# Streaming only the 64 query columns a level uses in the tree products of a gated linear recurrence

## The chip, the cores and the metric

The kernel runs on one core of one Trainium2 chip. The metric is the device time of one execution in microseconds (us); for a kernel it is the median of its runs.

## The reference, cut to what matters

One transformer block on a sequence of 1024 tokens of width 1024, all in float32: an RMS norm, one input projection, a sparse attention mixer (8 heads of 64), a gated linear recurrence (4 heads, keys and values of 128, chunks of 64 tokens in the reference), an output projection, and an MLP of width 4096. The change lies in the recurrence:

```python
def step(state, xs):                      # one chunk of C tokens, per head
    qc, kc, vc, lc = xs                   # lc = log of the forget gate f, kc = 1 - f
    bc = jnp.cumsum(lc, axis=2)
    diff = jnp.where(causal[:, :, None], bc[:, :, :, None, :] - bc[:, :, None, :, :], -jnp.inf)
    a = jnp.einsum('bhtd,bhsd,bhtsd->bhts', qc, kc, jnp.exp(diff))
    o = jnp.einsum('bhtd,bhdv->bhtv', qc * jnp.exp(bc), state) + jnp.einsum('bhts,bhsv->bhtv', a, vc)
    b_last = bc[:, :, -1:, :]
    state = jnp.exp(b_last[:, :, 0, :])[..., None] * state + jnp.einsum('bhsd,bhsv->bhdv', kc * jnp.exp(b_last - bc), vc)
    return state, o
```

The matrix `a` says how strongly query t of a chunk sees key s, with the product of all gates between s and t in it, separately for each of the 128 features.

## The kernel before, in words

The stages follow each other: input projection (to about 332 us of the profiled execution), attention (to about 648 us), the recurrence (to about 746 us), then output projection and MLP. Each engine (TensorE, called PE in the profile, with its weight loads PEld; VectorE, DVE; ScalarE, ACT; GpSimd, POOL; SyncE, SP) has its own instruction stream in program order, and they meet at semaphores.

The recurrence takes chunks of 128 tokens (8 chunks, `NT`), 4 heads (`HH`). It never forms the 128x128x128 decay. It builds `a` as a binary tree of seven levels. At level l the tokens are cut into blocks of b = 2^l; two neighbouring blocks form a pair, and the level fills in those entries of `a` whose key lies in the first block of a pair and whose query lies in the second. For that, `hgrn_q` (`hq`) and `hgrn_k` (`hk`) hold queries and keys that already have the gates up to the pair's border multiplied in. Features stand on the partitions and tokens on the free axis, so one product of a chunk and head is one TensorE matmul: stationary operand `hk[:, c, head]` (128 features x 128 keys), moving operand `hq[:, c, head]` (128 features x 128 queries), result 128 keys x 128 queries in PSUM. The operands are float32, and each such matmul stands in the trace as two weight loads and two matmuls, so 16 records are one pair of chunks (2 chunks x 4 heads x 2), which fills two PSUM banks.

- Units. A unit `u` is one pair of chunks `cp` at one level, or on the diagonal: `level_unit(l, cp)` = 4 + 4 l + cp; units 0 to 3 are the diagonal. `pair_banks(u)` gives unit u two of the eight banks, in a ring of 4 units (`A_RING`). The diagonal products (moving operand `fm`, called `hgrn_qf`) come first, 64 records, then 7 levels x 4 units x 16 = 448 records (L2122, called at L2146).
- Waits of PE ahead of a unit of level l: the bank pair must have been merged (`A_dve` or `A_act`, unit u - 4), and for every second unit `q_up` and `k_up`, which say that VectorE has multiplied the gates of level l - 1 into `hq` and `hk` of half the chunks (`grp`). The two units of one half are called a group below: 32 records.
- VectorE, for each level and half: wait for the two units of the level (`A_full`), then multiply the gates into the second blocks of `hq` (L1589) and the first blocks of `hk` (L1590), combine the gates (L1591), and for levels 0 to 3 merge the two units into `hgrn_A` with a predicated copy (L1599). That copy reads only the columns of second blocks, `[:, :, :, b:2 * b]`.
- ScalarE merges levels 4 to 6 with plain copies (L1164), again only from second blocks' columns.
- After level 6, PE transposes `hk` (L2157) and runs the chunks one after the other: state products (L2190) and outputs (L2167, L2168).

The helper that the change uses existed before and VectorE used it at L1586 and L1587:

```python
def blocks_of(ap, b):
    v = ap.rearrange("p (n c) -> p n c", c=2 * b)
    return v[:, :, 0:b], v[:, :, b:2 * b]
```

Of the kernel before, what the change touches and what calls it, by code (L numbers as in the profile page):

```python
# [31 lines left out]
P = 128  # L32
# [11 lines left out]
HH = 4  # L44
# [210 lines left out]
def program(nc, x, attn_norm, w_in, q_norm, k_norm, cmp_pe_k, cmp_w1_k, cmp_w2_k, cmp_pe_v, cmp_w1_v,  # L255
# [5 lines left out]
    def sb(name, shape, dt, offset=None):  # L261
        if offset is None:
            n = 2 if dt == BF16 else 4
            for k in shape[1:]:
                n *= k
            n = (n + 31) // 32 * 32
            offset = at["small"]
            at["small"] += n
        return nc.alloc_sbuf_tensor_at(name, list(shape), dt, offset=base + offset)
# [37 lines left out]
    hk = sb("hgrn_k", [P, NT, BW], F32, 0)  # L307
    hq = sb("hgrn_q", [P, NT, BW], F32, 16384)
# [263 lines left out]
    def root_act(act, bufs, width):  # L572

        sums, _, log, root = bufs
        n = roots["act"] = roots["act"] + 1
        act.activation(log, sums, ACT.Ln, bias=eps[:, 0:1], scale=1.0 / width).then_inc(logs_ready, 1)
        act.wait_ge(logs_ready, n)
        act.activation(root, log, ACT.Exp, scale=-0.5).then_inc(root_ready, 1)
# [67 lines left out]
# [4 lines that stand above are left out]
# [13 lines left out]
    def level_unit(l, cp):  # L663

        return 4 + 4 * l + cp

    def pair_banks(u):

        return ps[:, 2 * (u % A_RING):2 * (u % A_RING) + 2, :].rearrange("p a x -> p (a x)")
# [122 lines left out]
    with nc.Block() as block:  # L792
# [565 lines left out]
        def _(dve):  # L1358
# [216 lines left out]
            for l in range(len(LEVELS)):  # L1575
                b = 1 << l
                for grp in range(2):
# [5 lines left out]
                    else:  # L1583
                        dve.wait_ge(q1_done, 4)
                        dve.wait_ge(k_done, 4)
                    _, q2 = blocks_of(flat(hq[:, 4 * grp:4 * grp + 4, :]), b)  # L1586
                    k1, _ = blocks_of(flat(hk[:, 4 * grp:4 * grp + 4, :]), b)  # L1587
                    f_ = products(l, grp).rearrange("p (n c) -> p n c", c=2)
# [303 lines left out]
        def _(pe):  # L1892
            pe.wait_ge(e_loaded, 80)
            nc.tensor.transpose(ps[:, 7, 0:GAIN_ROWS], gain_rows[:], eye[0:GAIN_ROWS, 0:GAIN_ROWS]).then_inc(gainsT, 1)
            for t in range(NT // 2):
                pe.wait_ge(x_loaded[t], 16)
                for k in range(KC):
                    if t == 0 and k == 7:
                        pe.wait_ge(gains_out, 1)
                    ins = nc.tensor.transpose(ps[:, k, t * P:(t + 1) * P], x_in[:, t, k * P:(k + 1) * P], eye[:])  # L1900
                    if t == 3:
                        ins.then_inc(rowsT_done, 1)
            for k in range(KC):
                pe.wait_ge(rows_low, k + 1)
                for t in range(NT // 2, NT):
                    if k == 0:
                        pe.wait_ge(x_loaded[t], 16)
                    ins = nc.tensor.transpose(ps[:, k, (t % 4) * P:(t % 4 + 1) * P], x_in[:, t, k * P:(k + 1) * P], eye[:])
# [208 lines left out]

            def product(u, c, rhs):  # L2120
                for h in range(HH):
                    ins = nc.tensor.matmul(pair_banks(u)[:, (HH * (c % 2) + h) * P:(HH * (c % 2) + h + 1) * P],  # L2122
                                           hk[:, c, h * P:(h + 1) * P], rhs(h), start=True, stop=True)
                return ins

            for cp in range(4):
                pe.wait_ge(k_done, cp + 1)
                for c in range(2 * cp, 2 * cp + 2):
                    ins = product(cp, c, lambda h: fm[:, 0, c, h, :])
                ins.then_inc(A_full, 1)  # L2130
            for l in range(len(LEVELS)):
                b = 1 << l
                for cp in range(4):
                    u = level_unit(l, cp)
                    if l == 0:
                        pe.wait_ge(q1_done, cp + 1)
                    elif cp % 2 == 0:
                        pe.wait_ge(q_up, 2 * (l - 1) + cp // 2 + 1)
                        pe.wait_ge(k_up, 2 * (l - 1) + cp // 2 + 1)
                    old = u - A_RING + 1  # L2140
                    if old > MERGED_BY_DVE:
                        pe.wait_ge(A_act, old - MERGED_BY_DVE)
                    else:
                        pe.wait_ge(A_dve, old)
                    for c in range(2 * cp, 2 * cp + 2):
                        ins = product(u, c, lambda h: hq[:, c, h * P:(h + 1) * P])  # L2146
                    ins.then_inc(A_full, 1)

            def kT(c):
# [31 lines left out]
            for c in range(NT):  # L2181
                if c < 3:
                    kT(c + 4)
                if c < NT - 1:
# [3 lines left out]
                    for h in range(HH):  # L2188
                        cols = slice(h * P, (h + 1) * P)
                        ins = nc.tensor.matmul(ps[:, c % 2, cols], hKT[:, c, cols], hv[:, 0, c, cols], start=True, stop=True)  # L2190
# [109 lines left out]
            for k in range(last):  # L2300
                g, c = divmod(k, NCPS)
# [36 lines left out]
```

## Time and profile before

| What | Value |
|---|---|
| median of 3 runs | 1470.96 us (1465.0 to 1474.64) |
| the profiled execution's own time | 1472.83 us |
| its span in the trace | 1471.0 us |
| PE busy, PEld busy | 1428.5 us (97%), 1222.5 us (83%) |
| DVE busy, ACT busy | 870.2 us (59%), 623.0 us (42%) |
| mean granted TensorE clock | 0.992 of full |

The span is the time from the first to the last instruction of the profiled execution, and 1.8 us lie around it. Times of rows count from the span's start. PE's busy time includes pipelined matmuls whose modelled ends overlap the next one's start; how fast PE gets on is read from the distance between starts. PEclk is the granted clock: 1.00 is 2.4 GHz and 0.50 is 1.2 GHz.

### The profile page before, as it was taken

The numbers are of one execution on the slowest core, as the hardware profiler recorded it, in microseconds if no ns is written. First come the engines' busy times: TensorE is split into PE (matmuls) and PEld (weight loads), VectorE is DVE, ScalarE is ACT, GpSimd is POOL, SyncE is SP. The second block draws the span as 40 slices with busy tenths as digits, with TensorE's granted clock in tenths as the row PEclk, the third lists the DMA queues.
The fourth block names the chain that finished last, engine by engine and source line by source line (L and its number), as shares of the span: only waits on it lengthen the run. The fifth ranks groups of instructions, "written<-read, shape, count | busy, mean of one in ns | idle before, by whom it ended". The sixth has DMA issues, their size and how long they took to land.

```text
span 1471.0 us, 21626 instructions
## 1 busy us (share of the span) xinstructions
PE 1428.5 (97%) x7950; PEld 1222.5 (83%) x7950; DVE 870.2 (59%) x1630; ACT 623.0 (42%) x1235; POOL 161.5 (11%) x178
## 2 busy tenths in 40 slices
PE   7999999999999999998999989999999999999999
PEld 6888888878888888898987868888888788888887
DVE  3002681106666776669784586666666598569764
ACT  5014302215554545460440467755555554444441
POOL 2433343521000000000242000000000000000000
PEclk9999999998999999999999999999999999999999
DMA  5211114200000000012011014444444966643332
GB/s 176 61 47 51 51 36 122 72 7 1 1 2 1 1 2 1 1 44 115 30 51 36 30 36 165 158 152 157 157 158 139 327 206 191 213 127 100 93 115 86
DMA packets 78254, 129.42 MB, mean 88 GB/s; under 512 B 8973, under 2 KB 26826, under 8 KB 78154
## 3 DMA queue, kind: packets, MB, share of 16 engines
q1 hardware_dynamic: 77968, 128.01, 27.3%
q8 instruction: 63, 1.03, 0.3%
q14 instruction: 37, 0.30, 0.1%
q10 hardware_dynamic: 186, 0.08, 0.0%
HBM read 94.51 MB, written 33.55 MB: 87 GB/s over the span
## 4 chain that ended last, share of the span: by engine, by line
PE 87%; DVE 8%; ACT 2%; issue 2%; DMA 1%; SPq 0%; DVEq 0%; ACTq 0%
PE ps L518 64%; PE ps L2102 6%; PE ps L2062 4%; PE ps L2077 4%; PE ps L2122 3%; PE ps L2096 1%; PE ps L2046 1%; PE ps L1935 1%; DVE negmax L1492 1%; PE ps L2067 1%; DMA x_in<-in_x_dram 1%; PE ps L757 1%; DVE q_stack L1485 1%; PE ps L624 0%; DVE hgrn_A L1599 0%
## 5 line engine op out<-in xcount | busy, mean ns | idle before, releaser
L518 PE MATMUL ps<-mlp_w_high,hidden_high 128*128 128x512 f32 x448 | 174.3, 389 | 0.0
L518 PE MATMUL ps<-mlp_w_low,hidden_high 128*128 128x512 f32 x448 | 174.3, 389 | 0.0
L518 PE MATMUL ps<-mlp_w_high,hidden_low 128*128 128x512 f32 x448 | 174.3, 389 | 0.0
L518 PE MATMUL ps<-w_high,hT_high 128*128 128x512 f32 (+1 forms) x448 | 170.5, 380 | 0.8 <-ACT cmp_v L1072 0.7
L518 PE MATMUL ps<-w_low,hT_high 128*128 128x512 f32 (+1 forms) x448 | 168.1, 375 | 0.0
L518 PE MATMUL ps<-w_high,hT_low 128*128 128x512 f32 (+1 forms) x448 | 168.0, 375 | 0.0
L2102 PE MATMUL ps<-nsa,probs_T 128*128 128x64 f32 x1056 | 138.2, 275 | 0.0
L1664 DVE TENSOR_TENSOR mlp_w_low<-mlp_w_raw,mlp_w_high 128x512 fp32r<-128x512 f32 x112 | 77.1, 690 | 98.3 <-ACT mlp_w_high L1200 98.3
L1299 ACT ACTIVATE mlp_w_high<-mlp_w_raw 128x512 fp32r<-128x512 f32 x112 | 70.6, 630 | 148.2 <-PE ps L518 148.2
L2102 PEld LDWEIGHTS ps<-nsa,probs_T 128*128 128x128 f32 x1056 | 129.5, 193 | 0.0
L1744 DVE TENSOR_TENSOR mlp_w_low<-mlp_w_raw,mlp_w_high 128x512 fp32r<-128x512 f32 x112 | 77.0, 688 | 65.8 <-ACT mlp_w_high L1299 65.8
L518 PE MATMUL ps<-x1T_t_high,mlp_w_high 128*128 128x512 f32 x256 | 100.8, 394 | 6.2 <-issue 5.4
L1122 ACT ACTIVATE probs<-ps,negmax 128x640 f32<-128x640 f32 (+7 forms) x128 | 89.4, 699 | 29.5 <-DVE negmax L1492 29.5
L518 PE MATMUL ps<-x1T_t_high,mlp_w_low 128*128 128x512 f32 x256 | 100.6, 393 | 0.0
L518 PE MATMUL ps<-x1T_t_low,mlp_w_high 128*128 128x512 f32 x256 | 100.6, 393 | 0.0
L1492 DVE TENSOR_REDUCE negmax<-ps 128x1 f32<-128x640 f32 (+7 forms) x128 | 89.3, 701 | 18.5 <-PE ps L2067 17.9
L518 PEld LDWEIGHTS ps<-mlp_w_high,hidden_low 128*128 128x128 f32 x448 | 84.1, 188 | 17.6
L518 PEld LDWEIGHTS ps<-mlp_w_high,hidden_high 128*128 128x128 f32 x448 | 84.1, 188 | 17.5
L518 PEld LDWEIGHTS ps<-mlp_w_low,hidden_high 128*128 128x128 f32 x448 | 84.1, 188 | 17.3
L518 PEld LDWEIGHTS ps<-w_high,hT_high 128*128 128x128 f32 x448 | 84.1, 188 | 17.1 <-DVE hT_low L1364 1.6
L1134 ACT ACTIVATE probs_T<-ps 128x128 f32<-128x128 f32 (+3 forms) x129 | 53.2, 430 | 102.9 <-PE ps L2077 101.7
L518 PEld LDWEIGHTS ps<-w_high,hT_low 128*128 128x128 f32 x448 | 84.1, 188 | 15.2
(234 smaller groups left out, 2893.1 us busy)
## 6 DMA issues: line engine op xcount, KB each, us to landing
hidden_raw<-hidden_pieces SPq DMA_DIRECT2D x112, 256.0 KB, 2.7
mlp_w_raw<-in_w_mlp_in_dram SPq DMA_DIRECT2D x32, 512.0 KB, 4.2
hidden_pieces<-hidden SPq DMA_DIRECT2D x64, 256.0 KB, 2.8
mlp_w_raw<-in_w_mlp_out_dram SPq DMA_DIRECT2D x64, 256.0 KB, 4.3
w_raw<-in_w_in_dram SPq DMA_DIRECT2D x56, 256.0 KB, 2.7
hidden_pieces<-hidden_s SPq DMA_DIRECT2D x48, 256.0 KB, 2.2
x_in<-in_x_dram SPq DMA_DIRECT2D x8, 512.0 KB, 7.3
w_raw<-in_w_out_dram SPq DMA_DIRECT2D x16, 256.0 KB, 2.8
```

Source lines behind the costliest of these rows:

```text
L518: ins = nc.tensor.matmul(out_ap, a_hl[i], b_hl[j], start=first and n == 0, stop=last and n == 2, skip_group_check=onto_a_sum_already_read)
L757: ins = nc.tensor.transpose(ps[:, bank0 + f, q * P:(q + 1) * P], source(f, q), eye[:])
L1122: act.activation(o, sv, ACT.Exp, bias=negmax[:, j % NEGMAX:j % NEGMAX + 1], accum_out=rsums[:, hh % 2, t, int(kind == "win"):int(kind == " ...
L1134: act.activation(pT[:, it.groups[m]["pt"], 0:n], ps[:, T_BANK + m % 2, 0:n], ACT.Copy).then_inc(t_act, 1)
L1299: act.activation(ring_slot(W2R, k)[0], w2_source(k), ACT.Copy).then_inc(w2_highs, 1)
L1492: dve.tensor_reduce(negmax[:, j % NEGMAX:j % NEGMAX + 1], sv, AX if len(sv.shape) == 2 else mybir.AxisListType.XY, ALU.max, negate=True).t ...
L1664: dve.tensor_tensor(W1_L[:, s, :, :], w1_source(*IN_ORDER[k]), W1_H[:, s, :, :].bitcast(F32), ALU.subtract)\
L1744: dve.tensor_tensor(wl, w2_source(k), wh.bitcast(F32), ALU.subtract).then_inc(w2_lows, 1)
L2062: ins = nc.tensor.matmul(o, QT[:, hh % 2, t * P:(t + 1) * P], k_[:, br, hh // HPG:hh // HPG + 1, tiles[0] * P + b * (w // nb):tiles[0] * P ...
L2077: ins = nc.tensor.transpose(ps[:, T_BANK + m % 2, q * P:(q + 1) * P], probs[:, j % P_SLOTS, (u["first"] + q) * P:(u["first"] + q + 1) * P] ...
L2102: ins = nc.tensor.matmul(ps[:, O_BANK + it.pair(j) % 2, c:c + DK], lhs, nsa[:, tiles[n], v0 + hh // HPG * DK:v0 + (hh // HPG + 1) * DK], s ...
L2122: ins = nc.tensor.matmul(pair_banks(u)[:, (HH * (c % 2) + h) * P:(HH * (c % 2) + h + 1) * P], hk[:, c, h * P:(h + 1) * P], rhs(h), start=T ...
```

## The change

The products of the levels get a function that narrows both the moving operand and the place in the bank: `blocks_of(ap, b)[1]`, the second block of each pair. A level then streams 64 of the 128 query columns: every second column at level 0, runs of 2, 4, 8, 16, 32 at levels 1 to 5, and the last 64 in one run at level 6. The stationary operand stays 128 x 128. The columns in between are no longer written; VectorE and ScalarE did not read them at these levels. The diagonal products still stream all 128. The number of instructions, their order and all waits are unchanged.

```diff
-            def product(u, c, rhs):
+            def product(u, c, rhs, part=lambda ap: ap):
                 for h in range(HH):
-                    ins = nc.tensor.matmul(pair_banks(u)[:, (HH * (c % 2) + h) * P:(HH * (c % 2) + h + 1) * P],
-                                           hk[:, c, h * P:(h + 1) * P], rhs(h), start=True, stop=True)
+                    ins = nc.tensor.matmul(part(pair_banks(u)[:, (HH * (c % 2) + h) * P:(HH * (c % 2) + h + 1) * P]),
+                                           hk[:, c, h * P:(h + 1) * P], part(rhs(h)), start=True, stop=True)
                 return ins
...
-                        ins = product(u, c, lambda h: hq[:, c, h * P:(h + 1) * P])
+                        ins = product(u, c, lambda h: hq[:, c, h * P:(h + 1) * P], lambda ap: blocks_of(ap, b)[1])
```

## Rows read from the trace of the kernel before

**Rows 1.** The page: busy time by engine, and the granted clock in 40 slices

```profile
PE 1428.5 (97%) x7950; PEld 1222.5 (83%) x7950; DVE 870.2 (59%) x1630; ACT 623.0 (42%) x1235; POOL 161.5 (11%) x178
...
PEclk9999999998999999999999999999999999999999
```

**Rows 2.** The chain that ended last, 600 to 800 us: start, us, what

```profile
649.62 12.63 PE ps L2122 x96
...
687.33 3.81 PE ps L2122 x32
691.14 25.45 PE ps L2122 x224
716.62 1.22 DVE hgrn_q L1589
```

**Rows 3.** Timeline of 644 to 735 us: PE's records of the recurrence

```profile
658.49 7.31 PE L2122 MATMUL ps<-hgrn_q,hgrn_k 128*128 128x128 f32 x64
...
667.16 3.81 PE L2122 MATMUL ps<-hgrn_q,hgrn_k 128*128 128x128 f32 x32 [1.36 <-DVE hgrn_A L1599]
...
672.83 3.81 PE L2122 MATMUL ps<-hgrn_q,hgrn_k 128*128 128x128 f32 x32 [1.85 <-DVE hgrn_A L1599]
...
677.95 3.81 PE L2122 MATMUL ps<-hgrn_q,hgrn_k 128*128 128x128 f32 x32 [1.31 <-DVE hgrn_A L1599]
...
687.33 29.25 PE L2122 MATMUL ps<-hgrn_q,hgrn_k 128*128 128x128 f32 x256 [0.45 <-DVE hgrn_A L1599]
...
717.35 1.94 PE L2157 MATMUL ps<-eye,hgrn_k 128*128 128x128 f32 x16 [0.77 <-ACT hgrn_A L1164]
```

**Rows 4.** Groups of 658 to 720 us, shapes apart: busy us, mean ns, idle before

```profile
L1599 DVE COPY_PREDICATED hgrn_A<-tree_masks,ps 128x512 f32<-128x512 int32 x16 | 14.8, 997 | 0.0
L1589 DVE TENSOR_TENSOR hgrn_q<-hgrn_q,hgrn_f 128x1024 f32<-128x1024 f32 x12 | 14.7, 1226 | 4.7 <-PE ps L2122 4.7
L1590 DVE TENSOR_TENSOR hgrn_k<-hgrn_k,hgrn_f 128x1024 f32<-128x1024 f32 x12 | 14.5, 1211 | 0.0
L1164 ACT ACTIVATE hgrn_A<-ps 16x128 f32<-16x128 f32 x16 | 4.3, 269 | 38.5 <-DVE hgrn_A L1599 38.3
```

**Rows 5.** The chain of 640 to 650 us: attention's last matmuls of 64 columns

```profile
644.93 2.87 PE ps L2102 x26
```

**Rows 6.** The compression's matmuls, moving operand read with a step of 8 elements

```profile
237.63 7.71 PE L1935 MATMUL ps<-cmp_tokens,cmp_w 128*128 128x130 f32 x32
```

**Rows 7.** Busy time of each stretch, granted clock (PEclk), DMA share, GB/s

```profile
336.50:340.00 3.50, 3.50 (x19) 3.47 (x18) 0.10 (x1) 0.12 (x1) 0.16 (x1) 0.56 0.00 0
340.00:344.20 4.20, 3.36 (x17) 2.80 (x17) 2.79 (x6) 1.99 (x7) 0.00 (x0) 0.50 0.01 4
344.20:347.70 3.50, 3.50 (x19) 3.50 (x19) 0.71 (x3) 0.58 (x3) 0.00 (x0) 0.50 0.00 0
347.70:350.60 2.90, 2.90 (x14) 2.28 (x15) 1.72 (x4) 1.41 (x5) 0.00 (x0) 0.50 0.01 3
350.60:354.00 3.40, 3.40 (x27) 2.84 (x27) 3.22 (x11) 1.98 (x6) 0.00 (x0) 1.00 0.00 0
644.70:647.80 3.10, 3.08 (x29) 2.94 (x26) 0.57 (x4) 0.77 (x2) 0.00 (x0) 1.00 0.00 0
647.80:650.90 3.10, 1.28 (x11) 1.28 (x12) 2.96 (x5) 2.39 (x3) 0.00 (x0) 1.00 0.43 128
650.90:654.30 3.40, 3.40 (x18) 3.40 (x18) 3.34 (x4) 3.37 (x5) 0.00 (x0) 0.51 0.93 308
654.30:658.40 4.10, 4.10 (x39) 4.10 (x38) 2.91 (x3) 4.10 (x15) 0.00 (x0) 0.99 0.10 35
...
672.80:677.90 5.10, 3.81 (x32) 3.65 (x32) 5.10 (x6) 0.00 (x0) 0.00 (x0) 1.00 0.96 374
```

**Rows 8.** Timeline of 341 to 351 us: attention's compressed outputs, 64 columns

```profile
344.28 3.62 PE L2096 MATMUL ps<-cmp_v,probs_T 128*128 128x64 f32 x16
...
347.69 0.42 PE L2077 MATMUL ps<-eye,probs 128*128 128x128 f32 x1
```

## The prediction

> **What bounds the kernel now.** I read four views in this order. The page first: PE is busy for 97% of the span, weight loads for 83%, VectorE for 59%, and the granted clock is full nearly everywhere [rows 1]. That says only that PE's pace matters somewhere. The chain that ended last says where: around the recurrence's products it runs over PE from 649.62 for 96 records (64 of the diagonal, 32 of level 0), then over VectorE, and from 687.33 over PE alone for 32 + 224 records, up to VectorE's gate products at 716.62 [rows 2]. The timeline shows why. From 667 to 687 us each group of 32 PE records takes 3.8 us and then PE idles 1.3 to 1.9 us until a merge of VectorE's frees banks [rows 3]; VectorE has no idle time before its merges, and 4.7 us in all before its gate products [rows 4]. So levels 0 to 2 are VectorE's, though PE's groups take nearly as long, and levels 3 to 6 are PE's: 256 records in 29.25 us. There are 448 such records, 51 us of PE's time, in one stage of 1471 us; the change touches nothing else.
>
> **The pace of these records.** 224 records took 25.45 us [rows 2], 114 ns each, with 128 columns streamed. What does one of 64 columns take? Attention has it, with the same kinds of operands (float32, stationary 128x128): 26 records in 2.87 us, 110 ns [rows 5]. The few ns between them are the waits between units. Half the columns buy nothing, so what limits the pace is not the stream but the load of the stationary operand, which the change leaves alone. The Trainium skill, page "TensorE: Matmul & The Clock Gate", section "LDWEIGHTS (loading the stationary operand)", gives 128 / 1.2 = 107 ns for such a load whatever the moving operand; an estimate by it says the same as the row of 64 columns.
>
> **Term 1: the stream of the 448 records at full clock.** Removed: 64 columns each. Gain 0 by rows 5, as the weight load covers it. If that cover were gone, the most to gain is the idle time that VectorE has before its gate products, 4.7 us [rows 4], since VectorE is then what is late next. At the ends of groups the last result may land some tens of ns sooner; only two such ends lie on the chain where PE hands over for good (662 and 717 us), so I count 0.1 us, which is nothing.
>
> **Term 2: the strided reads and writes.** The nearest row for reading is the compression's matmul: its moving operand has a step of 8 elements, and 32 records of 130 columns take 7.71 us [rows 6]. Taking off the last one's tail of about 0.4 us, 31 steps take 7.3 us, 235 ns each or 1.81 ns per column. 64 such columns would take 116 ns, 4 ns over the 112 of the load. That row has a wider step than any level here (2 elements at level 0, runs from level 1 on), so it is the upper end for reading: 448 x 4 ns = 1.8 us. The lower end is 0: at level 0 the 64 columns touch the same stretch of memory as 128 contiguous ones, and those keep pace with the load. I take 0, because levels 2 to 6 have runs of four columns or more. No row shows a strided write into PSUM. Bound it below by 0 (no reason lets it speed anything up), above by a doubling to about 224 ns at level 0 alone, where single columns are written: 32 records lie on the chain ahead of 662 us, and the other 32 delay level 1; together 64 x 0.11 = 7 us at most, of which the 1.36 us of idle time after it [rows 3] hides some, so about 5.5. I take 0 here too.
>
> **Term 3: the clock.** This is the part where I expect the time to move. The granted clock has two levels in this trace, and it is worth asking what PE had done before each move.
> - It fell from 1.00 to 0.50 near 337 us and near 651 us [rows 7]. Ahead of the second lie 26 records of 64 columns (full clock, though thinly streamed) and then 1.85 us without work between the stages; it fell 3.2 us after the idle time began, with PE busy again with 128-column records.
> - At 0.50, 3.5 us of PE 100% busy did not bring it back: in 344.2 to 347.7 PE and its loads were busy all the time, with 16 records of 64 columns, and the clock stayed at 0.50, through the next stretch too; it was back at 1.00 after matmuls of 384 columns [rows 7, 8].
> - In 650.9 to 654.3 PE was just as busy, at half clock, with 128-column records, and the clock came back at once [rows 7].
> So a PE that is busy with loads is not enough; it is the streamed columns that tell these stretches apart. In the levels, idle gaps of 1.3 to 1.9 us today lie between groups of 128 columns, and the clock holds (672.8 to 677.9 is 1.00 with 3.81 of 5.1 us busy) [rows 7]. After the change the same gaps lie between groups of 64 columns, which is what PE did ahead of the fall at 651. I expect the clock to fall after the gap that ends level 0 (it starts near 665.8): by the 3.2 us seen above, near 669. Then every group is 64-column work at half clock, the very pattern of 344.2 to 347.7 that did not bring the clock back. It should stay at 0.50 until the products end.
>
> What that costs. At half clock the 64-column records stand 3.41 us / 16 = 213 ns apart (344.28 to 347.69) [rows 8]; with the 2 ns for waits between units (114 against 112) 215. Group 1 of level 1 starts at 667.16 at full clock and falls on the way: about 16 records at 112 and 16 at 213 take 5.2 us, so it ends by 672.4, ahead of 672.83, when the banks of the next group come free [rows 3]: nothing lost yet. From there 11 groups are left, 352 records x 0.215 = 75.7 us. VectorE needs per group 2.4 us for the two gate products (1.2 each) and up to 2.4 for two merges or none [rows 4], less than the 6.9 that PE takes, and each group of PE needs only gate products that can run during the other half's group. So no wait is left in it, and PE ends at 672.83 + 75.7 = 748.5 in place of 716.6: +31.9 us. Everything behind waits for it: VectorE's last gate products, the transposes, the chunks. The loads of the output projection's weights are not late today and have only more time.
>
> After the products come transposes and state products of 128 columns, which brought the clock back in 3.4 us at 651. I give it 5 us here, as PE has two short waits at the start [rows 3]; at half pace that loses 2.5 us.
>
> **The sum.** 0 + 0 + 31.9 + 2.5 = +34.4 us. The profiled execution took 1472.83 us (span 1471.0), so it would be 1507.2, span 1505.4. The median of the runs, 1470.96, is 1.9 us lower; on it the forecast is 1505.4 us.
>
> **Rival A: the clock holds.** Then only terms 1 and 2 are left, and the weight load hides both: 1471 us. For it: the gaps keep their length, PE's busy share stays, and the clock held through long runs of 64-column records in attention [rows 5, 7]. Against it: those runs had no idle time, and where one came (647.8) the clock fell. The Trainium skill (same page, "Why this matters for your kernels") names only idle gaps between bursts as what costs the clock, longer ones than any here; by that rule the change would give 1471. The trace disagrees at 651, where a gap of 1.85 us was enough. Chance 0.10.
>
> **Rival B: strided access is dear and the clock is not the matter.** If level 0 alone doubles, +5.5 us, 1476. If all levels but the last, which is one run, went to twice the time, 11 groups less level 6's two would run at about 224: 9 x 32 x 0.11 = +32, near 1503, at full clock. It decides from the point where a record passes the 112 ns of the load; reading by rows 6 gives 116. The Trainium skill has a rule that speaks for it: "SBUF — State Buffer" on cachelines says that any non-contiguous PSUM access slows matmuls significantly. No row here shows it for writes. Chance 0.06, half of it near 1476.
>
> **Rival C: faster, because the stream matters after all.** Then PE finishes the groups of levels 3 to 6 early and VectorE binds: at most its 4.7 us of idle time [rows 4], 1466. Against it rows 5. Chance 0.02.
>
> **How the numbers follow.** The forecast, clock lost until the products end, has 0.82. Its own range: below, if the clock comes back for part of the way (half of the levels spared, 1488); above, level 0 doubled (+5.5), the clock already lost ahead of level 0's first group (32 records x 0.10 = 3.3), a slower return behind (+3), reading at its upper end at levels 0 and 1 (+1): 1518. I take 1488 to 1518; it holds 0.78 of the 0.82, and with the dear half of rival B 0.81 in all. By over 1%, 14.7 us (about what a measurement of this kernel can tell from no change), it is slower in the forecast's case and in the dear half of B, less a little for a clock that comes back soon: 0.83. Within 1%: A, cheap B, C and that little: 0.16. Faster by over 1%: 0.01, since nothing seen could give 15 us.
>
> **What the changed profile would show.** The granted clock at 0.50 from near 669 to near 753 and nowhere else anew; PE's product records 213 ns apart there and 112 in level 0; the idle times of PE before groups gone from level 2 on, and those of VectorE before its gate products grown to 3 us and more each; the stage's end some 32 us later and the stages behind it unchanged in length. Term 1 is right if level 0's 64 records still take about 7.3 us. If that group takes 14 us at clock 1.00, B was right. If the clock stays at 1.00 with the gaps in place, A was, and my reading of the two falls was wrong: something else than columns tells those stretches apart.

## The result

The changed kernel takes 1507.45 us (median, 1502.68 to 1509.85) against 1472.34 us of the kernel before (1465.0 to 1474.97). The ratio is 1.0245, with a 95% interval of 1.0222 to 1.0269: 2.5% slower. The forecast was 1505.4 us, range 1488 to 1518. The profiled execution took 1504.32 us with a span of 1502.4 us, 31.4 more than before.

The page has the same 21626 instructions. PE's busy time rose from 1428.5 to 1466.6 us although it streams fewer columns, VectorE's stayed (871.3 against 870.2), and two slices of the span have about half the clock where [rows 1] had full:

```profile
PE 1466.6 (98%) x7950; PEld 1261.3 (84%) x7950; DVE 871.3 (58%) x1630; ACT 622.9 (41%) x1235; POOL 161.4 (11%) x178
...
PEclk9999999999999999985599999999999999999999
```

PE's timeline of 653 to 751 us in the changed kernel shows the recurrence's products:

```profile
653.81 7.26 PE L2122 MATMUL ps<-hgrn_q,hgrn_k 128*128 128x64 f32 x64
662.43 82.16 PE L2122 MATMUL ps<-hgrn_q,hgrn_k 128*128 128x64 f32 x384 [1.36 <-DVE hgrn_A L1599]
745.36 4.50 PE L2157 MATMUL ps<-eye,hgrn_k 128*128 128x128 f32 x20 [0.77 <-ACT hgrn_A L1164]
```

Level 0's 64 records take 7.26 us where they took 7.31 [rows 3]: at full clock half the columns buy nothing. Then the four groups with idle time ahead and the run of 256 of [rows 3] have become one run of 384 records in 82.16 us, 214 ns each, without an idle moment. The chain of this stretch follows PE all the way where it followed VectorE for 25 us before [rows 2]:

```profile
662.43 82.17 PE ps L2122 x384
744.62 0.60 ACT hgrn_A L1164
```

The windows of the changed kernel (start and end, length, PE busy, PEld busy, DVE, ACT, POOL, granted clock, DMA share, GB/s) show the clock and what PE did around its moves:

```profile
644.80:648.00 3.20, 1.44 (x12) 1.44 (x13) 3.12 (x5) 2.55 (x3) 0.00 (x0) 1.00 0.43 150
653.80:661.00 7.20, 7.20 (x66) 7.13 (x64) 4.79 (x6) 3.76 (x11) 0.00 (x0) 1.00 0.00 1
661.00:661.80 0.80, 0.07 (x1) 0.00 (x0) 0.80 (x2) 0.00 (x0) 0.00 (x0) 1.00 0.00 0
661.80:668.70 6.90, 6.27 (x30) 6.30 (x30) 6.90 (x7) 0.00 (x0) 0.00 (x0) 0.50 0.13 45
668.70:744.60 75.90, 75.88 (x356) 75.69 (x355) 39.34 (x51) 9.05 (x27) 0.00 (x0) 0.50 0.13 52
744.60:750.60 6.00, 5.25 (x25) 5.28 (x26) 5.59 (x8) 0.59 (x1) 3.17 (x4) 0.50 0.04 9
750.60:765.00 14.40, 14.40 (x131) 14.40 (x131) 9.44 (x27) 4.76 (x9) 4.18 (x5) 1.00 0.21 71
```

Level 0 runs at full clock. In the 1.36 us of idle time behind it the clock falls to 0.50 (1.2 GHz) and stays there for 89 us, with PE busy nearly all the time (its only idle moment of note is the 0.77 us ahead of the transposes). It comes back 6 us after the last product, once 128-column transposes and state products run. VectorE, which had 4.7 us of idle time before its gate products [rows 4], now waits 36.5 us (groups of 658 to 750 us):

```profile
L1589 DVE TENSOR_TENSOR hgrn_q<-hgrn_q,hgrn_f 128x1024 f32<-128x1024 f32 x12 | 14.7, 1225 | 36.5 <-PE ps L2122 36.5
```

**The 31.4 us, stage by stage,** from the starts of PE's records in the two profiled executions:

| Stretch | before | changed | difference |
|---|---|---|---|
| start to level 0's first record | 658.49 | 653.81 | -4.68 |
| level 0 to the first transpose (L2157) | 58.86 | 91.55 | +32.69 |
| to the output projection's first matmul (L518) | 29.14 | 30.97 | +1.83 |
| to the MLP's first matmul | 98.27 | 99.88 | +1.61 |
| to the end | 626.2 | 626.2 | 0 |

The first row is not the change's: attention ended 3.1 us earlier in that execution, where the clock's fall at 337 us lasted 6.8 us in place of 13.7; and the fall at 651 us [rows 7] did not happen (1.00 from 644.8 to 661 above), though PE did the same work. The fourth is a short fall of the clock behind idle time in the output projection. The work and the idle time are the same in both kernels, but in one of the two profiles the clock fell:

```profile
770.00:778.00 8.00, 5.95 (x28) 4.66 (x27) 7.66 (x18) 0.00 (x0) 1.96 (x2) 1.00 0.21 66
778.00:790.00 12.00, 12.00 (x62) 10.21 (x61) 5.52 (x8) 2.42 (x4) 1.82 (x2) 1.00 0.01 1
```

These are windows of the kernel before; the same stretch of the changed kernel:

```profile
800.00:808.00 8.00, 5.95 (x29) 4.70 (x28) 7.48 (x17) 0.00 (x0) 1.96 (x2) 1.00 0.20 66
808.00:820.00 12.00, 12.00 (x55) 10.23 (x54) 5.61 (x8) 2.59 (x4) 0.46 (x1) 0.86 0.01 1
```

Such a fall is worth 1.6 us. Whether it belongs to the change is open: of the thirteen profiles of this document seven have it (this one, contig64, narrow012, wide3, square6, tiles056 and tilesall), and none of the five whose levels take the 58.8 to 58.9 us of the kernel before. The stage itself is the measure below: "levels" is the time from level 0's first record to the first transpose, 58.86 us before and 91.55 after.

### The profile page after: what moved, and what is told of

It is laid out like the page before. It is cut to its first block, busy times and chain, and to the rows that moved or that the text cites. A ratio compares the mean times of both kernels' runs of the same rounds, so it can differ in the third digit from the quotient of the medians.

```text
span 1502.4 us, 21626 instructions
## 1 busy us (share of the span) xinstructions
PE 1466.6 (98%) x7950; PEld 1261.3 (84%) x7950; DVE 871.3 (58%) x1630; ACT 622.9 (41%) x1235; POOL 161.4 (11%) x178
## 4 chain that ended last, share of the span: by engine, by line
PE 89%; DVE 6%; ACT 2%; issue 2%; DMA 1%; SPq 0%; ACTq 0%; DVEq 0%
PE ps L518 63%; PE ps L2122 6%; PE ps L2102 6%; PE ps L2062 4%; PE ps L2077 3%; PE ps L1935 1%; PE ps L2096 1%; PE ps L2046 1%; DVE negmax L1492 1%; PE ps L2067 1%; DMA x_in<-in_x_dram 1%; PE ps L757 1%; DVE q_stack L1485 1%; PE ps L624 0%; DVE hgrn_vg L1633 0%
## 5 line engine op out<-in xcount | busy, mean ns | idle before, releaser
L518 PE MATMUL ps<-mlp_w_high,hidden_high 128*128 128x512 f32 x448 | 174.4, 389 | 0.0
L518 PE MATMUL ps<-mlp_w_high,hidden_low 128*128 128x512 f32 x448 | 174.4, 389 | 0.0
L518 PE MATMUL ps<-mlp_w_low,hidden_high 128*128 128x512 f32 x448 | 174.4, 389 | 0.0
L518 PE MATMUL ps<-w_high,hT_high 128*128 128x512 f32 (+1 forms) x448 | 171.1, 382 | 0.8 <-ACT cmp_v L1072 0.7
L518 PE MATMUL ps<-w_low,hT_high 128*128 128x512 f32 (+1 forms) x448 | 168.6, 376 | 0.0
L518 PE MATMUL ps<-w_high,hT_low 128*128 128x512 f32 (+1 forms) x448 | 168.3, 376 | 0.0
L518 PE MATMUL ps<-x1T_t_high,mlp_w_high 128*128 128x512 f32 x256 | 100.8, 394 | 6.3 <-issue 5.4
L518 PE MATMUL ps<-x1T_t_high,mlp_w_low 128*128 128x512 f32 x256 | 100.6, 393 | 0.0
L518 PE MATMUL ps<-x1T_t_low,mlp_w_high 128*128 128x512 f32 x256 | 100.6, 393 | 0.0
L518 PEld LDWEIGHTS ps<-w_high,hT_high 128*128 128x128 f32 x448 | 84.5, 189 | 17.1 <-DVE hT_low L1364 1.6
L518 PEld LDWEIGHTS ps<-mlp_w_high,hidden_high 128*128 128x128 f32 x448 | 84.1, 188 | 17.6
L518 PEld LDWEIGHTS ps<-mlp_w_high,hidden_low 128*128 128x128 f32 x448 | 84.1, 188 | 17.5
L518 PEld LDWEIGHTS ps<-mlp_w_low,hidden_high 128*128 128x128 f32 x448 | 84.1, 188 | 17.3
L518 PEld LDWEIGHTS ps<-w_high,hT_low 128*128 128x128 f32 x448 | 84.4, 188 | 15.2
L518 PEld LDWEIGHTS ps<-w_low,hT_high 128*128 128x128 f32 x448 | 84.5, 189 | 14.6
```

What stands on the lines that cost most here:

```text
L518: ins = nc.tensor.matmul(out_ap, a_hl[i], b_hl[j], start=first and n == 0, stop=last and n == 2, skip_group_check=onto_a_sum_already_read)
```

## The experiments

All runs were compared with the kernel before on the same chip; the kernel before took 1468.65, 1472.64, 1474.53 and 1472.69 us in the four sets.

**Is it the stride or the number of columns?** Two kernels split the change in two. The first keeps 64 columns and takes the stride away; it leaves out most entries of levels 0 to 5:

```diff
-ins = product(u, c, lambda h: hq[:, c, h * P:(h + 1) * P], lambda ap: blocks_of(ap, b)[1])
+ins = product(u, c, lambda h: hq[:, c, h * P:(h + 1) * P], lambda ap: ap[:, P // 2:P])
```

> At every level the products stream the last 64 of the 128 query columns in one contiguous run, into the last 64 columns of the bank, so most entries of the matrix are wrong at levels 0 to 5; instructions and waits are those of the changed kernel. Theory of columns (the clock falls because few columns are streamed around the idle time after level 0, and stays down): as slow as the changed kernel, +35 us on the kernel before, about 1507, with 213 ns between records from level 1 on at clock 0.50. Theory of strides (the strided view is what slows the records): no stride is left, so the time is that of the kernel before, 1472, at clock 1.00.

Measured: 1507.34 us, ratio 1.0259 (1.0221 to 1.0296). Levels 91.55 us, to the hundredth those of the changed kernel:

```profile
651.32 7.26 PE L2122 MATMUL ps<-hgrn_q,hgrn_k 128*128 128x64 f32 x64
659.94 82.15 PE L2122 MATMUL ps<-hgrn_q,hgrn_k 128*128 128x64 f32 x384 [1.36 <-DVE hgrn_A L1599]
```

The second keeps the strides and streams all 128 columns:

```diff
+ins = product(u, c, lambda h: hq[:, c, h * P:(h + 1) * P], lambda ap: ap.rearrange("p (n a c) -> p a n c", a=2, c=b))
```

> At every level all 128 columns are streamed, first blocks of all pairs first and then second blocks, each with the stride of the level, and written to the same places, so the result is the same. Theory of columns: the time of the kernel before, 1472 (within 3 us), clock 1.00, 112 ns between records, at level 0 too. Theory of strides: slower by at least as much as the changed kernel, 1507 or more, with long records at clock 1.00.

Measured: 1469.76 us, ratio 1.0001 (0.9978 to 1.0024), levels 58.93 us. PE's timeline of this kernel, level 0, then the groups of levels 1 and 2:

```profile
662.27 7.42 PE L2122 MATMUL ps<-hgrn_q,hgrn_k 128*128 128x128 f32 x64
671.00 3.87 PE L2122 MATMUL ps<-hgrn_q,hgrn_k 128*128 128x128 f32 x32 [1.31 <-DVE hgrn_A L1599]
676.66 3.86 PE L2122 MATMUL ps<-hgrn_q,hgrn_k 128*128 128x128 f32 x32 [1.80 <-DVE hgrn_A L1599]
681.78 3.81 PE L2122 MATMUL ps<-hgrn_q,hgrn_k 128*128 128x128 f32 x32 [1.26 <-DVE hgrn_A L1599]
```

Against 7.31, 3.81 and 3.81 us [rows 3] the stride costs 0.11 us on 64 records at level 0, 0.05 to 0.06 on 32 at level 1, and nothing from level 2 on; the idle time behind takes it up. That holds for reading and writing together. With 64 columns it costs nothing at all: level 0 takes 7.26 us in the changed kernel and in contig64. The strides are cleared as a cause; the number of columns is it. (They are not shown to be free. The output projection's records of 512 columns, of the form fp32r, start 0.227 us apart at full clock; at that pace 128 columns take 57 ns, and twice that, 113 ns, would barely show beside the 112 ns of the load. These are estimates, and level 0 here runs at 113.5 ns against 111.7 before, so a stride that doubles the stream is not excluded.)

**Does it take idle time as well as few columns?** 64 columns at levels 4 to 6 only, where PE has no idle time:

```diff
+... lambda ap: blocks_of(ap, b)[1] if l >= 4 else ap)
```

> 64 columns only at levels 4 to 6, where PE has no idle time; 128 at levels 0 to 3. Theory that narrow streams cost the clock only together with idle time: clock stays 1.00, time of the kernel before, 1472 (within 2 us), since the weight load hides the stream. Rival, that narrow streams alone cost the clock: 192 records x 0.102 us = +20 and some 2 us for the return, 1494.

Measured: 1472.29 us, ratio 1.0014 (0.9988 to 1.004), levels 58.79 us; the clock held (windows of this kernel):

```profile
681.60:710.80 29.20, 29.16 (x256) 28.89 (x256) 24.54 (x36) 9.04 (x27) 0.00 (x0) 1.00 0.00 1
```

From level 3 on (`l >= 3`), with 0.45 us of idle time ahead of the first narrow group:

> The changed kernel with 128 columns at levels 0 to 2: 64 columns from level 3 on. Ahead of level 3 PE idles 0.45 us, ahead of its second group 0.2 us, later never. Theory (it takes narrow records and more than a short idle time together): clock stays 1.00, 1472. Rival (0.45 us of idle time among narrow records is enough): it falls near 690 us and stays down to the end of the levels, some 230 records x 0.102 = +23 and 2 for the return, 1497.

Measured: 1472.67 us, ratio 0.9995 (0.997 to 1.002), levels 58.81 us at clock 1.00. Narrow records by themselves neither cost the clock nor gain a thing. The other way round, 64 columns at levels 0 to 2 only:

```diff
+... lambda ap: blocks_of(ap, b)[1] if l < 3 else ap)
```

> 64 columns only at levels 0 to 2, where PE idles between groups; 128 at levels 3 to 6. Theory of columns: the clock falls after level 0, groups of levels 1 and 2 take 128 x 0.213 = 27.3 us from 667.2 on, 7.1 us longer than to 687.3, then 128-column records at half clock bring it back in 3 to 7 us, which costs 2.5 us: +9.6, 1482 (1478 to 1485). Rival, that a clock once lost stays lost as long as this stage lasts whatever is streamed: +34, 1506.

Measured: 1482.32 us, ratio 1.0068 (1.0041 to 1.0096), which is +10.0 us; levels 66.31 us, +7.45, and the profile has the 1.6 us in the output projection too. Windows:

```profile
658.90:666.20 7.30, 7.30 (x67) 7.20 (x65) 4.66 (x5) 2.48 (x6) 0.00 (x0) 1.00 0.00 1
666.20:670.30 4.10, 2.74 (x25) 2.73 (x25) 4.10 (x5) 0.00 (x0) 0.00 (x0) 1.00 0.00 0
670.30:697.50 27.20, 26.14 (x124) 25.98 (x123) 21.78 (x24) 0.00 (x0) 0.00 (x0) 0.50 0.40 155
697.50:700.90 3.40, 3.40 (x31) 3.40 (x31) 1.88 (x3) 0.00 (x0) 0.00 (x0) 0.98 0.00 0
```

Here the clock fell 4 us after the idle time began, not within it as in the changed kernel's profile, so where exactly it falls varies. It came back at 697.6, in the 128-column records of level 3. The rival, that it stays lost for the stage, would have given 1506.

64 columns at level 0 alone (`l == 0`):

> 64 columns at level 0 alone, 128 at levels 1 to 6. Theory of columns: the idle time behind level 0 (1.36 us) has narrow records only ahead of it; the clock falls in some executions and in others not; where it falls, level 1's 128-column records at half clock bring it back in 3 to 7 us. The first group of level 1 can lose 32 x 0.1 = 3 us, hidden in part by the 1.85 us of idle time behind it: +0 to +4, 1472 to 1476. Theory of strides with single columns dear at level 0: +5.5, 1478, at clock 1.00.

Measured: 1471.24 us, ratio 0.9998 (0.9973 to 1.0022), levels 58.82 us. The clock did fall in the profile (0.50 from 668.0 to 671.4) and the first group of level 1 took 5.44 us in place of 3.81, but the idle time behind it shrank from 1.85 to 0.23 us:

```profile
667.35 5.44 PE L2122 MATMUL ps<-hgrn_q,hgrn_k 128*128 128x128 f32 x32 [1.36 <-DVE hgrn_A L1599]
673.02 3.81 PE L2122 MATMUL ps<-hgrn_q,hgrn_k 128*128 128x128 f32 x32 [0.23 <-DVE hgrn_A L1599]
```

A fall that wide records mend at once is hidden by the very idle time that caused it. What costs is that nothing mends it.

**Can narrow records hold the clock that they can't bring back?** The changed kernel, with 128 columns at level 3 alone:

```diff
+... lambda ap: ap if l == 3 else blocks_of(ap, b)[1])
```

> The changed kernel with 128 columns at level 3 alone; 64 at all other levels. Theory (narrow records without idle time hold a full clock, but cannot bring it back): the clock falls after level 0, comes back within level 3, and stays up through levels 4 to 6: +9.6, 1482 (1478 to 1486). Rival (narrow records lose the clock by themselves, sooner or later): it falls again in levels 4 to 6, up to 192 x 0.102 = +20 more, 1502.

Measured: 1482.93 us, ratio 1.0081 (1.0053 to 1.0109), +11.9 us; levels 67.21 us. Windows, the last of them all narrow but for the end of level 3:

```profile
670.00:694.50 24.50, 24.50 (x118) 24.50 (x117) 20.14 (x21) 0.00 (x0) 0.00 (x0) 0.50 0.44 172
694.50:700.80 6.30, 6.30 (x31) 6.30 (x31) 3.90 (x5) 0.00 (x0) 0.00 (x0) 0.50 0.00 0
700.80:727.00 26.20, 26.17 (x234) 26.02 (x232) 20.36 (x30) 9.05 (x27) 0.00 (x0) 1.00 0.01 1
```

The same narrow records, PE busy all the time in both, stay at 0.50 until 128-column records come and at 1.00 behind them. Widening one level of the seven gives back 23 of the changed kernel's 35 us.

**Is the weight load what sets the pace?** Then it must pay to load less. The kernel before, but level 6 loads only the 64 keys that it uses:

```diff
+if half:
+    out_, k_, q_ = out_[0:P // 2, P // 2:P], k_[:, 0:P // 2], q_[:, P // 2:P]
 ins = nc.tensor.matmul(out_, k_, q_, start=True, stop=True)
```

> The kernel before, but level 6 loads only the 64 key columns that it uses as stationary operand and streams only its 64 query columns, result 64 x 64; the other entries were never read. Theory (the weight load sets the pace, about 1/1.2 ns per column): records of level 6 stand about 56 to 60 ns apart, clock 1.00 as columns are streamed just as densely; PE saves 1.8 us in the last group and some 1 us in the one before, where VectorE's gate products come late: -3 us, 1469. Rival (a fixed cost per record): no change in pace, 1472. Rival (fewer cells at work let the clock fall): 64 records at twice the pace, no gain or +2 us.

Measured: 1471.36 us, ratio 1.0007 (0.9986 to 1.0028). The last group's timeline row:

```profile
710.60 2.05 PE L2126 MATMUL ps<-hgrn_q,hgrn_k 128*64 128x64 f32 x32 [0.49 <-issue]
```

Less a last record's 0.22 us, 31 steps take 1.83 us: 59 ns in place of 112. Levels took 56.29 us, 2.6 less, as expected; in the whole time nothing is seen, and this profile has 1.6 us of it given back in the output projection, where the clock fell. It also fell inside the levels, from 672.1 to 675.5, with 128 columns in every record; the wide records brought it back and the idle time behind took up the loss. So the idle time of 1.85 us can cost the clock even among wide records. Level 5 as well, in two products of 32 keys by 32 queries:

```diff
+for s0 in range(0, P, 2 * n):          # n = 32 at level 5, 64 at level 6
+    ins = nc.tensor.matmul(out_[s0:s0 + n, s0 + n:s0 + 2 * n], k_[:, s0:s0 + n], q_[:, s0 + n:s0 + 2 * n],
+                           start=True, stop=True)
```

> The kernel before, but at level 6 a product loads 64 key columns and streams 64 query columns, and at level 5 it is two products of 32 key by 32 query columns each; all that is read later is computed. In the profile of the run with level 6 alone its records stood 58 ns apart and the levels took 55.5 in place of 58.1 us. Theory: two loads of 32 cost about one of 64, so level 5 gets the same pace; VectorE's gate products (2.4 us a group) then bind levels 5 and 6: levels 54 us or a little less, -4 us, 1468. Rival (a floor per record above 30 ns): level 5 no faster than 16 records x 112 a unit, time as with level 6 alone, 1470. Rival (the idle time that faster groups leave lets the clock fall): levels 60 us or more, 1474.

Measured: 1468.83 us, ratio 0.9979 (0.9954 to 1.0003), not quite clear of no change; levels 53.97 us, 4.9 less. Records of 32 by 32 are faster than expected, and VectorE's idle time is gone:

```profile
700.79 1.21 PE L2128 MATMUL ps<-hgrn_q,hgrn_k 128*32 128x32 f32 x64
...
L1589 DVE TENSOR_TENSOR hgrn_q<-hgrn_q,hgrn_f 128x1024 f32<-128x1024 f32 x12 | 14.8, 1230 | 0.3 <-PE ps L2125 0.3
```

These are one row of the timeline and one of the groups. VectorE binds now, and PE waits up to 1.4 us between the groups of levels 5 and 6, with the clock at 1.00 there. At level 1 it fell in this profile too, from 672.2 to 675.6 and again just behind the idle time of 1.85 us: that makes two of the six profiles with 128-column records at levels 0 and 1.

**A version that beats both.** As square56, with the diagonal and level 0 in four tiles of 32 by 32 per chunk and head; then levels 1 to 4 in such tiles too.

```diff
+ins = product(cp, c, lambda h: fm[:, 0, c, h, :], (32, 0))                # the diagonal
+... (b, b) if l >= 5 else (32, 0) if l == 0 else (P, P))                  # tiles056; tilesall: else (32, 0) for all
```

> As square56, and the diagonal and level 0 use four tiles of 32 keys by 32 queries per chunk and head in place of 128 by 128 (all entries that are read later lie in them); levels 1 to 4 stay 128 by 128. Theory: tiles of 32 stand 16 ns apart as in square56, so 256 records of the diagonal take 4.1 us in place of 7.2 and 256 of level 0 as much; VectorE then starts level 0's gate products as soon as its diagonal merges are over, near 658 in place of 662.3; from the end of attention to the end of the products 56 to 58 us in place of 67.0 (60.5 in square56): -9 us, 1464. Rival: so few streamed columns with idle time let the clock fall at once; level 1's 128-column records pay for it until it is back, +3 us: 1467.

Measured: 1466.69 us, ratio 0.996 (0.9941 to 0.998): 0.4% faster than the kernel before. The theory's 1464 was missed by 3 us, and the number is the rival's 1467: the clock fell at once, at 651.6, and was down until 668.7. But level 1's 128-column records did not pay for it. Its two groups took 9.47 us from start to end, as they did before (667.16 to 676.64); the idle time between them was used up. From the diagonal's first product to the first transpose it took 60.8 us (649.53 to 710.36) against 61.2 in square56 (649.80 to 711.02); to the end of the products, which is what 56 to 58 was said of, 60.1 against 60.5. PE's timeline shows where it went: PE is through three quarters of the diagonal early and then idles 2.88 us, for which the profile names no other engine ("issue"):

```profile
649.53 0.76 PE L2127 MATMUL ps<-hgrn_qf,hgrn_k 128*32 128x32 f32 x64 [1.84 <-ACT hgrn_k L1144]
655.57 1.01 PE L2127 MATMUL ps<-hgrn_qf,hgrn_k 128*32 128x32 f32 x58 [2.88 <-issue]
```

Two more such idle times follow in level 0 (1.55 and 1.77 us), and VectorE starts its first gate product at 660.23, after 2.17 us of idle time, not near 658. The trace points to the fetch of the instructions, four times as many here: each of the three idle times ends 1.2 to 1.5 us after an instruction packet of 16 KB has landed (654.1, 657.8 and 661.4 us, against PE's starts at 655.57, 659.05 and 662.76). No run isolates it. What the tiles add to square56 is not clear of noise, as the two intervals overlap.

> As tiles056, and levels 1 to 4 in tiles of 32 by 32 too. Theory: the clock falls and stays at 0.50 to the end of the products, but a group's 128 records at twice 16 ns take 4.1 us, and VectorE's work per group is 5.7 us at level 0 and 3.8 at level 3, so nearly all of it is hidden; levels 4 to 6, where VectorE has 2.5 us a group, pay up to 1.6 us for each of level 4's two groups, and the return of the clock behind the products costs 2 us: 1467. Rival: at half clock tiles no longer overlap in pairs and stand 50 ns or more apart, a group takes 6.8 us and PE binds: 1480 or more.

Measured: 1467.78 us, ratio 0.9961 (0.9944 to 0.9979). Levels 54.26 us, though the clock was at 0.50 from 656.7 to 707.9 (windows, PE alone: busy, clock, DMA share, GB/s):

```profile
658.00:675.00 17.00, 8.02 (x492) 0.50 0.19 65
675.00:700.00 25.00, 13.37 (x768) 0.50 0.33 130
```

At half clock a group's 128 tile records take 2.2 us (level 1's first two groups 2.22 and 2.15 us in the timeline), less than the 4.1 expected and less than VectorE needs, so here a lost clock costs almost nothing: PE is not the bound.

This profile also limits what wide3 shows. The clock came back at 707.9, with no 128-column record since attention: only tiles of 32 columns, and then 13 records of 64 keys by 64 queries, which stood 107 ns apart at half clock and 59 behind the return:

```profile
703.99 1.92 PE L2127 MATMUL ps<-hgrn_q,hgrn_k 128*32 128x32 f32 x64 [1.06 <-issue]
706.39 4.59 PE L2127 MATMUL ps<-hgrn_q,hgrn_k 128*64 128x64 f32 x64 [0.48 <-issue]
```

So it is not the width of a record by itself. What did not bring the clock back in the levels of any profile is 64 columns behind a load of 128, 213 ns apart at half clock.

## Why the prediction was right

**Term 1 (the stream at full clock, 0).** Right: 7.26 against 7.31 us at level 0, and levels of 58.79 and 58.81 us with narrow records at full clock. The reason, the weight load, is shown by the pair of paces: 128 by 64 at 112 ns, like 128 by 128, and 64 by 64 at 59.

**Term 2 (strides, 0; bounds 0 to 5.5 and 1.8).** Right: nothing with 64 columns (7.26 us at level 0 with and without the stride), and with 128 columns 0.11 us at level 0 and 0.05 to 0.06 per group at level 1. The Trainium skill's rule ("SBUF — State Buffer", on cachelines) that any non-contiguous PSUM access slows matmuls significantly shows as no more than 2 ns per record at single float32 columns with a step of two, read and write together. That is where the load sets the pace and can cover a slower stream; no run here shows the stream alone.

**Term 3 (the clock, +31.9).** Right in mechanism, and near in size: +32.7 us. The pace of 213 ns, read from rows of 64-column records at half clock [rows 8], was met (214). The fall came within the idle time, at about 661.9, 0.8 us after it began, and not 3.2 us after; in contig64 it came 1.2 us after, in narrow0 2, in wide3 2.3 and in narrow012 4. I had the first group of level 1 lose nothing, as idle time lies behind it. At half clock from its start that group takes 6.9 us, 3.1 more than before, and the idle time covers only 1.85 of them. That is where term 3 was short, by 1.2 us, of which the pace, 214 in place of 215 ns, gives some back: 0.8 in all.

**The return of the clock (+2.5).** It took 6 us behind the products and cost 1.8. The 1.6 us in the output projection was not in the sum, and the prediction had said that the clock would be down nowhere else anew. No profile of the kernel before shows that fall, so it may be a part of the change's price. Some of the closeness is luck: term 3 came out 0.8 us over the forecast and the return 0.7 under it. The three together are 36.1 us; the ratio of 1.0245 is 36.1 us too, with an interval from 33 to 40 that cannot tell 34.4 from 36.1.

**The rivals.** A (the clock holds) fell with the profile, B (strides) with contig64 and strided128, C (the stream matters) with narrow456. That it takes idle time and narrow records together for a fall that lasts, which the prediction read from one pair of stretches, is shown by narrow456 and narrow3456 on the one side and narrow012 on the other (idle time alone made the clock fall in square6 and square56, and wide records mended it); that 64-column records behind a load of 128 do not bring the clock back but do hold it, by wide3. That all narrow records fail to bring it back would be too much: tilesall's 64 by 64 did not need wide ones.

## What to carry to other kernels

Before cutting the columns of a matmul, look at whether the stationary load sets its pace; if it does, nothing is gained, and the stream that is cut away may be what keeps TensorE's clock up through the idle times around it: here it cost 2.5%. Look in the trace for places where the clock fell or failed to return with PE busy, and compare what was streamed there with what the change would leave. To gain from a mask that uses a part of the columns, cut the loaded side as well: 64 by 64 ran at 59 ns where 128 by 64 and 128 by 128 both ran at 112. How much of it reaches the whole time depends on what waits next: VectorE here, so that square56's 4.9 us in the levels was not clear of noise in the total.

## What the runs showed of the hardware that I had not expected

Float32 records of 32 by 32, each with its own load, stood much closer than the 59 ns of 64 by 64, and how close went with how many strips of 32 rows of the result they took turns in. With two strips (level 5) they stood 16 ns apart at full clock (64 in 1.21 us, less the last one's 0.2) and 27 at half (64 in 1.92 us, tilesall). With four strips they stood 9 ns apart at full clock (64 in 0.76 us, tiles056) and 13 to 16 at half (127 in 1.93 us, tiles056, and 128 in 2.22, tilesall).

The clock fell within 0.8 us of the start of an idle time in one profile and 4 us after it in another, and with the same work it fell or held in different executions: behind attention's end, in seven of the eleven profiles that do the diagonal as the kernel before does; and in the output projection, in seven of all thirteen. A gap of 1.85 us among 128-column records, harmless in the profile before, cost the clock in square6 and in square56, for 3.4 us each.
